# Two blocks of a transformer on one core: the second block's token mixer, cut by token tiles and moved partly beside the first block's expert rows

## The reference

```
h = gelu(einsum('bthkd,btd->bthk', u_tab[idx], xi))
out = einsum('bthk,bthkd->btd', gate * h, v_tab[idx])
```

```
proj = h @ w_in                                     # 1024 x 8208
cb, cc, cu, q, k, v, f_logit, g_conv, g_att = split_cols(proj)
y_conv = short_conv(cb, cc, cu, conv_w, conv_b) @ w_conv_out
s = q @ k.T * scale + (cum[query] - cum[key])       # cum = cumsum(log_sigmoid(f_logit + b)), causal softmax, 16 heads of 64
y_att = o @ w_att_out
return (sigmoid(g_conv) * y_conv + sigmoid(g_att) * y_att) @ w_out
```

## Time and profile before

| | us |
|---|---|
| median of 3 timed runs (2493.71 to 2498.93) | 2497.79 |
| the profiled execution's own time | 2491.84 |
| its span, first to last instruction | 2490.1 |
| PE busy / DVE busy / POOL busy / ACT busy | 1983.1 / 1100.6 / 977.0 / 421.6 |
| PE matmul L2031 (rows of `v`) | 983.7 |
| PE matmul L1840 (weights stationary) | 287.9 and 57.5 |
| HBM read | 857.64 MB |

### The profile page before, as it was taken

How to read it: one execution, slowest core, us unless ns; L and a number is a source line. 1 busy time by engine, 2 the same in 40 slices (tenths; PEclk the granted TensorE clock), 3 DMA queues, 4 the chain that set the end, 5 groups by cost and what they waited for, 6 DMA issues and landing times.

```text
span 2490.1 us, 21117 instructions
## 1 busy us (share of the span) xinstructions
PE 1983.1 (80%) x7462; PEld 1022.2 (41%) x7462; DVE 1100.6 (44%) x2634; ACT 421.6 (17%) x1107; POOL 977.0 (39%) x1059
## 2 busy tenths in 40 slices
PE   8837997779988779989777777789999975566555
PEld 4523552235444225435322222248887732222221
DVE  6579638952457954455975444421012130000001
ACT  2312411201311111311111111101023110000000
POOL 0036757774556775546777777600000000000000
PEclk9868999999999999999999999999989988887887
DMA  6279999999999999999999999966543589999996
GB/s 221 93 262 338 409 402 407 409 409 399 402 357 406 409 409 402 399 372 342 409 409 409 409 409 409 410 208 166 151 101 121 191 342 426 428 426 427 427 427 266
DMA packets 228318, 860.19 MB, mean 345 GB/s; under 512 B 26080, under 2 KB 26592, under 8 KB 216432
## 3 DMA queue, kind: packets, MB, share of 16 engines
q0 software_dynamic: 147456, 536.94, 54.8%
q1 hardware_dynamic: 77488, 312.04, 33.1%
q10 hardware_dynamic: 3264, 9.80, 1.0%
HBM read 857.64 MB, written 1.05 MB: 345 GB/s over the span
## 4 chain that ended last, share of the span: by engine, by line
PE 37%; DMA 28%; DVE 18%; POOL 8%; issue 5%; ACT 2%; SPq 1%; DVEq 0%; ACTq 0%
PE psum L1840 13%; DMA rows<-in_peer_v,idx 8%; PE psum L2031 8%; DVE rows L1051 7%; PE psum L1832 6%; DMA rows<-in_w_e_gate 5%; POOL rows L691 4%; DMA rows<-in_w_e_down 4%; POOL rows L703 4%; DMA rows<-in_peer_u,idx 4%; DMA rows<-in_w_e_up 3%; PE psum L2234 3%; DMA rows<-in_gla_w_in 2%; PE psum L2257 1%; DVE work L934 1%
## 5 line engine op out<-in xcount | busy, mean ns | idle before, releaser
L2031 PE MATMUL psum<-rows,diag 128*128 128x512 f32 x2024 | 983.7, 625 | 264.6 <-ACT diag L1559 136.7
L1051 DVE CUSTOM_DVE_ANT_0 rows<-rows,psum 128x1024 f32<-128x1024 f32 x512 | 614.8, 1220 | 294.0 <-DMA rows<-in_peer_u,idx 283.2
L2031 PEld LDWEIGHTS psum<-rows,diag 128*128 128x128 f32 x2024 | 370.1, 195 | 832.1 <-issue 508.2
L691 POOL DMA_INDIRECT rows<-in_peer_u,idx x512 | 489.5, 956 | 378.2 <-DVEq L728 144.7
L703 POOL DMA_INDIRECT rows<-in_peer_v,idx x512 | 483.7, 945 | 272.6 <-PE psum L2031 148.6
L1840 PE MATMUL psum<-work,rows 128*128 128x256 f32 (+1 forms) x1664 | 287.9, 335 | 0.7 <-ACT work L1378 0.7
L1840 PEld LDWEIGHTS psum<-work,rows 128*128 128x128 f32 x1664 | 260.4, 193 | 31.0 <-issue 5.8
L1559 ACT ACTIVATE diag<-ident,wgt 128x128 f32<-128x128 f32 x506 | 166.0, 389 | 332.1 <-DVE wgt L1059 332.1
L2234 PE MATMUL psum<-rows,work 128*32 128x512 f32 x896 | 136.2, 693 | 106.0 <-DMA kept<-in_w_e_up 46.4
L1321 DVE TENSOR_TENSOR work<-kept,psum 128x512 f32<-128x512 f32 x8 | 8.2, 1030 | 423.2 <-PE psum L2234 423.2
L1378 ACT ACTIVATE work<-psum 128x512 f32<-128x512 f32 (+4 forms) x158 | 81.2, 532 | 547.7 <-PE psum L1840 194.9
(11 more groups left out here) (309 smaller groups left out, 1342.9 us busy)
## 6 DMA issues: line engine op xcount, KB each, us to landing
rows<-in_w_e_up SPq DMA_DIRECT2D x28, 2048.0 KB, 20.1
rows<-in_w_e_gate SPq DMA_DIRECT2D x25, 2048.0 KB, 20.5
rows<-in_w_e_down SPq DMA_DIRECT2D x24, 2048.0 KB, 20.9
rows<-in_w_in SPq DMA_DIRECT2D x32, 1024.0 KB, 9.6
rows<-in_gla_w_in SPq DMA_DIRECT2D x24, 1024.0 KB, 18.4
rows<-in_peer_w_query SPq DMA_DIRECT2D x16, 1024.0 KB, 9.2
rows<-in_peer_u,idx POOLq DMA_INDIRECT x512, 11.7
rows<-in_peer_v,idx POOLq DMA_INDIRECT x512, 12.1
```

The source lines that it names most:

```text
L691: pool.indirect_dma_start(out=u_rows[:, n % RU, :], out_offset=None, in_=a["peer_u"][g // 2], in_offset=bass.IndirectOffsetOnAxis(ap=idx[: ...
L1051: V_.tensor_tensor_reduce(out=u, in0=u, in1=tokens, scale=1.0, scalar=0.0, op0=ALU.mult, op1=ALU.add, accum_out=hid[:, r:r + 1]).then_inc( ...
L2031: last = mm(psum[:, 6 + c, :], diag[:, at % DIAGS, :], v_rows[:, n % RV, c * BANK:(c + 1) * BANK], start=r == 0, stop=summed(n + 1) == sum ...
```

## The change

The stage "mixa" is gone, and "mix" now works on one token tile: ("mix", 0) stands beside the rows of group 3, ("mix", 1) behind them. Every matrix of the mixer is streamed once for each tile, in blocks of 512 columns with the tokens as the stationary side, so that the results stand token by feature; where the next product needs them the other way (`x`, `q`, `k`, `z`, `cb`, the attention's output and `m`), PE transposes them and ACT copies them. 20 blocks of 512 columns and the forget logits belong to each tile. The product of tile 0 with `w_out` is not made in ("mix", 0): it is made at the start of ("mix", 1), as `p0` and `p1`, beside the time in which DVE adds the last experts and norms tile 1. The forget sums are no longer a bias on DVE: each score bank gets a second product (one column of the identity, broadcast, times `cum` of 16 partitions), and DVE takes only the mask. `stage_rows` puts 4 rows behind each of the 20 blocks, 2 behind each set of transposes, 1 behind each `T` and `O` job of the attention and 1 behind `f`: 109 rows.

In ("mix", 1) ACT issues the four first gate matrices of "moe" at four places, behind `k0`, `v1`, `cu1` and `bT1`, after waits for all rows to be used. SP issues the first four up matrices behind the last job of the attention, the last use of ring slot 0, `o0` and `o1`; the final gain waits for `resid1`. SP no longer waits for `u_used`. The `w_out` product of tile 1 is cut in two halves of k over both banks. GpSimd's iota waits for `mT1`. The DVE work of the convolution is the same 24 instructions for each tile, on 128 columns.

```diff
@@ -41,13 +41,12 @@
 
 
 BEFORE = [("mla", 0), ("route", 0)]
-BESIDE = [[("mla", 1), ("route", 1)], [("gla", 0), ("route", 2)], [("gla", 1), ("route", 3)], [("mixa", 0)]]
-AFTER = [("mix", 0), ("moe", 0)]
+BESIDE = [[("mla", 1), ("route", 1)], [("gla", 0), ("route", 2)], [("gla", 1), ("route", 3)], [("mix", 0)]]
+AFTER = [("mix", 1), ("moe", 0)]
 STAGES = BEFORE + [key for beside in BESIDE for key in beside] + AFTER
 
 
-BETWEEN = [{-1: "gc0", 0: "gc1", 1: "gc2", 2: "gc3", 3: "ga0", 4: "ga1", 5: "ga2"},
-           {-1: "ga3", 0: "yc0", 1: "yc1", 3: "oT0_0", 4: "oT0_1"}]
...
-                + ["yc2"] + turned_jobs(1) + ["yc3"] + [f"ya{i}" for i in range(4)] + ["o00", "o10", "o01", "x00", "x01", "o11", "r0"])
+        jobs = (["x0", "x1", "f", "q0", "q1", "k0", "qT0", "qT1", "k1", "v0", "kT0", "kT1", "v1", "cc0", "cc1", "cu0", "cu1",
+                 "cb0", "zT0", "cb1", "zT1", "bT0", "bT1"]
+                + attention_jobs(v, BETWEEN) + ["yc1"] + turned_jobs(v) + ["ya0", "ya1", "mT0", "mT1"])
+        return ["p0", "p1"] + jobs + ["o0", "o1", "x00", "x01", "r0"] if v else jobs
...
-        return {"x01": 2}
+    if stage == "mix":
+        streamed = ["q", "k", "v", "cc", "cu", "cb", "gc", "ga", "yc", "ya"]
+        return {"x1": 2, "f": 1, "qT1": 2, "kT1": 2, "zT1": 2, "bT1": 2, "oT0_1": 2,
+                **{f"{m}{i}": 4 for m in streamed for i in range(2)},
+                **{f"{m}0_{g}": 1 for m in "TO" for g in range(H // 2)}}
     return {"x1": 2, "q": 3, "k": 3, "v0": 3, "v1": 3, "r0": 3, "r1": 3, "low": 1, "gate": 8, "kd": 1, "at": 1,
...
+            out += two("w_out", ["p0", "p1"])
         out.append(("w_in_2", 6 * D, FH, "f"))
-        for m, c in (("cc", 1), ("cu", 2), ("cb", 0), ("q", 3), ("k", 4)):
-            out += two("w_in_2", [f"{m}1", f"{m}3"], c * D)
-        for m, c in (("gc", 6), ("ga", 7)):
-            out += two("w_in_2", [f"{m}1", f"{m}3"], c * D + FH)
-        return out + two("w_conv_out", ["yc1", "yc3"]) + two("w_att_out", ["ya1", "ya3"]) + two("w_out", ["o01", "o11"])
+        for m, c in (("q", 3 * D), ("k", 4 * D), ("v", 5 * D), ("cc", D), ("cu", 2 * D), ("cb", 0),
+                     ("gc", 6 * D + FH), ("ga", 7 * D + FH)):
+            out += two("w_in_2", [f"{m}0", f"{m}1"], c)
+        out += two("w_conv_out", ["yc0", "yc1"]) + two("w_att_out", ["ya0", "ya1"])
+        return out + two("w_out", ["o0", "o1"]) if v else out
     return []
...
                     sp.dma_start(h[:, 1, :], a["x"][P:S, :]).then_inc(h_here[1], 16)
             for n, (key, (what, c0, cols, last, k0, kn)) in enumerate(PIECES):
-                if key == ("mix", 0) and PIECES[n - 1][0] != key:
-
-                    sp.wait_ge(u_used, NU)
                 if n >= NW:
 
                     old_key, old = PIECES[n - NW]
-                    sp.wait_ge(emptied, JOB[(("mix", 0) if old[0] == "mix_gain" else old_key) + (old[3],)])
+                    sp.wait_ge(emptied, JOB[old_key + (old[3],)])
...
+                if at == 4:
+                    sp.wait_ge(emptied, JOB[("mix", 1, "O1_7")])
...
 
-                    for e in (3, 0, 1, 2):
+                    sp.wait_ge(v_used, summed(NU))
+                    sp.wait_ge(v_taken, len(SHARED))
+                    for e in range(GANG):
                         first_free(GANG + e)
                         load_matrix(sp, i, odd, 1, e)
+                    sp.wait_ge(dve_step, STEP["dve"][("moe", 0, "resid1")])
                     sp.dma_start(fin_gain, a["norm_final_g_2"].to_broadcast([P, D])).then_inc(fin_ready, 16)
                 else:
...
                 V("cum", key)
-                V_.memset(x_z[:, :, 0:2], 0.0)
-                got(key, "cu3")
-                link(V_.tensor_tensor(x_z[:, :, 2:], x_cc, x_cu, ALU.mult))
-                for c in range(KD):
-                    link(V_.tensor_scalar(x_cc[:, c, :], x_z[:, c, 0:S], conv_w[:, 0, c:c + 1], conv_b[:, c:c + 1], ALU.mult, ALU.add))
...
                 V("convy", key)
 
-                got(key, f"fb{H // 2 - 1}")
...
+                if t:
+                    act.wait_ge(u_used, NU)
+                    act.wait_ge(v_used, summed(NU))
+                    act.wait_ge(v_taken, len(SHARED))
+                first_gate()
...
+                attend(key, t, x_S, x_pT, x_o, between)
...
+
+                def between(g):
+                    for name in BETWEEN.get(g, []):
+                        if name == "yc0":
+                            seen(key, "convy")
...
+
+                def score(g, banks, w):
+                    for e, hh in enumerate(heads_of(g)):
+                        half = slice(hh % 2 * FD, (hh % 2 + 1) * FD)
+                        mm(banks[e], x_qT[half, hh // 2, :], x_kT[half, hh // 2, 0:w], start=True, stop=False)
+                        pick = ident[0:FH, hh:hh + 1].to_broadcast([FH, P])
+                        last = mm(banks[e], pick, x_cum[0:FH, 0:w], start=False, stop=True)
+                    return last
+
+                if t:
+                    pe.wait_ge(u_used, NU)
+                    got(("mix", 0), "mT1")
+                    for i in range(2):
+                        tokens(f"p{i}", x_mT)
+                seen(key, "xn")
+                for i in range(2):
+                    turned("x", i, x_xn)
+                got(key, "x1")
                 w, bank = Weight(), open_bank(key, "f")
                 for k in range(KD):
-                    last = mm(bank[0:FH, 0:S], w.at(k), x_xT[:, k, :], start=k == 0, stop=k == KD - 1)
+                    last = mm(bank[0:FH, 0:P], w.at(k), x_xT[:, k, :], start=k == 0, stop=k == KD - 1)
                 close(key, "f", last)
-                for m in ("cc", "cu", "cb", "q", "k"):
-                    for i in range(4):
-                        quarter_T(m, i, x_xT)
+                for name in ("q0", "q1", "k0"):
+                    tokens(name)
+                got(key, "q1")
+                for i in range(2):
+                    turned("qT", i, x_q)
+                for name in ("k1", "v0"):
+                    tokens(name)
+                got(key, "k1")
+                for i in range(2):
+                    turned("kT", i, x_k)
+                for name in ("v1", "cc0", "cc1", "cu0", "cu1", "cb0"):
+                    tokens(name)
+                seen(key, "z")
+                turned("zT", 0, x_cc)
+                tokens("cb1")
+                turned("zT", 1, x_cc)
+                got(key, "cb1")
+                for i in range(2):
+                    turned("bT", i, x_cb)
                 seen(key, "cum")
...
+                attend(key, t, score, x_S, x_pT, lambda kt, hh: x_v[:, kt, hh * FD:(hh + 1) * FD], between)
+                tokens("yc1", x_bT)
+                turn(key, t, x_o)
+                got(key, f"oT{t}_1")
+                for i in range(2):
+                    tokens(f"ya{i}", x_oT)
+                seen(key, "m0")
+                turned("mT", 0, x_ya)
+                if t == 0:
+                    seen(key, "m1")
+                    turned("mT", 1, x_ya)
+                    return
+                got(key, "mT0")
+                ws = [Weight() for _ in range(2)]
+                outs = [open_bank(key, f"o{i}") for i in range(2)]
+
+                def out(i, ks):
+                    for k in ks:
+                        last = mm(outs[i], x_mT[:, k, :], ws[i].at(k), start=k == 0, stop=k == KD - 1)
+                    return last
+
+                for i in range(2):
+                    out(i, range(KD // 2))
+                seen(key, "m1")
+                turned("mT", 1, x_ya)
+                got(key, "mT1")
+                for i in range(2):
+                    close(key, f"o{i}", out(i, range(KD // 2, KD)))
                 seen(key, "resid0")
                 for i in range(2):
                     transposes(key, f"x0{i}", chunks(h[:, 0, :], i))
-                out(1, 1)
                 logits(key, 0)
 
             def logits(key, t):
```

More of the change, by code:

```diff
@@ L117, in stage_steps @@
             return ["xn", "abs", "b", "qd", "kd", "at", "state1", "on", "state2", "resid"]
-        if stage == "mixa":
-            return ["xn0"]
         if stage == "mix":
-            return (["xn1", "abs", "cum", "convy", "bias"] + attention_order(0) + attention_order(1)[:4] + ["n0"]
-                    + attention_order(1)[4:] + ["n1"] + [f"m{i}" for i in range(4)]
-                    + ["router", "resid0", "rstd0", "xn0"])
+            head = ["xn", "resid0"] if v else ["xn"]
+            tail = ["rstd0", "m0", "m1", "xn0"] if v else ["m0", "m1"]
+            return head + ["abs", "cum", "z", "convy"] + attention_order(v) + [f"n{v}"] + tail
         return ["resid1", "rstd1", "picked", "shift", "xn1", "keys", "sum0"]
@@ L151, in stage_banks @@
 def stage_banks(stage, v):
-    alone = stage in ("mix", "moe") or (stage, v) == ("mla", 0)
+    alone = (stage, v) in (("mla", 0), ("mix", 1), ("moe", 0))
     return NB if alone else NB_ROWS
@@ L711, in _ @@
```

(41 more changed lines are left out.)

327 lines of the change are left out of this document (133 added, 194 removed).

## The result

The changed kernel takes 2507.45 us (median of 6 runs, 2506.35 to 2511.33); the kernel before, on the same chip, 2498.43 (2493.71 to 2501.61). The ratio is 1.0039, 95% interval 1.0026 to 1.0052: slower by 0.4%, where 2493 was forecast. The profiled execution's span is 2504.5 us against 2490.1, 14.4 longer. The medians differ by 9.0 only: the profiled execution of the kernel before (2491.84) was faster than all six runs of this comparison, that of the changed kernel (2506.35) only 1.1 under its median.

The account below looks back on a forecast made before the run. It took DMA to bound rows and experts, PE the mixer. Group 3 +116, mixer behind it -123.6, step to the experts +3 gave -4.6: 2487.2 us profiled, 2493 as median; range 2466 to 2523.

Parts of the forecast that it names:

- A: Rows of group 3, beside ("mix", 0): the second reading of weights lengthens them by 116 us, bounds 103 to 129.
- rival R1: In group 3, weights cost what they cost in the GLA stage as a whole, 129 us: 2506, slower; chance 0.27.
- B: ("mix", 1), last row to last `w_out` product: 240 us instead of 363.6, so 123.6 us saved.
- rival R3: Granted clock of 0.79 in the 113 us of ("mix", 1) behind `cb1` adds 30 us: 2523; chance 0.10.
- stall: ("mix", 1), `q0` to `cb1`: PE waits 24 us for slow `w_in` weights, bounds 0 to 45.
- The tail: End of ("mix", 1) behind attention, from `yc1` to the products with `w_out`: 39.7 us.
- C: Step from the mixer into the experts: 3 us longer, between 0 and 8.
- Rival R2: Weights keep up in ("mix", 1), no stall, 24 us less: 2469; chance 0.23.

Follow-up runs that it names:

- the picks experiment: Changed kernel with the forget sums' product over all 128 partitions (`cum` zero in 112) instead of 16: 2501.11 us, ratio 1.0015.
- the version with wide picks: Kernel before, with its 32 forget-sum picks over 128 partitions instead of 16, `cum` set to zero first: 2489.92 us, ratio 0.9969.

## Why the prediction was wrong, step by step

**A held.** Group 3 grew by 115.0 us (forecast +116, bounds 103 to 129); the last row came at 1760.8 instead of 1758, the other 2.8 us having come ahead of group 3. The whole-stage price of 129 (rival R1) did not apply. Inside the term, 8.5 us are the row distance. The forecast named it only behind the rows, but the rate that it took from the earlier trace rows is of `w_in` and had it in.

**B is the step that failed:** 255.3 us behind the last row, not 240. Of the 15.3, attention is 11.8 (81.5, not 69.7). It was summed from the earlier trace rows ("32 picks took 10.70 us, 0.33 each, so a pair is 4.1"), as if only the picks were slow and everything else ran as in its rows. Where the clock falls, all that stands there is slow: 16 instructions of a block at 9.10 us instead of 7.03, scores at 1.22 instead of 0.70. With the picks over 128 partitions and the rest as it was, attention took the 69.6 us that the sum had. The mechanism stood in the text as rival R3 with 0.10, from the earlier trace rows, at 0.79 over 113 us and +30; it was 0.81 over 81.5 us and, by the picks experiment, 11.9 us, of which the picks themselves are 3.0 (14.2 against 11.2). What spoke against it, rows at 0.98 with TensorE at 78%, was a stretch of products over 128 partitions and said nothing of 16. The earlier trace rows together held the evidence: a granted clock of 0.86 with TensorE busy for all 50 us leaves waits out as the reason, and the block behind the picks took 9.77 us there against 7.17 for its like in the version with wide picks.

The stretch to the first scores took 132.9 us; the forecast's terms give about 130 (103 to `cb1`, 24 of stall, 3 for the last transposes). The stall was right in size, 21.0 us of waits and some 5 us of slower products behind them (busy 111.6 against 106.6 with fewer waits) for 24, and right in cause: reading from rows 4 KB apart nearly removes it (5.3 us of waits stay, 4.7 of them ahead of the forget product). That the size fits is partly luck: 7.5 of the 21.0 us stood ahead of the forget product, where the forecast had none, and 13.5 behind it.

The sentence of the Trainium skill that the forecast set against it (DMA: Bandwidth & Descriptors, section Latency and other measured facts: with 4 MiB from one partition's row to the next, 4 KiB more restore the rate) does not cover this stride. The page measured distances of 512 KiB and more between neighbouring partitions; in a piece of `w_in` neighbouring partitions read neighbouring rows, 32.8 KB apart, and the 4 MiB that the forecast compared lie between groups of 128 rows. The page has no figure for such a distance, and the forecast's reading of it, no loss, did not hold: 279 against 370 GB/s in two runs of the same pieces is one. The forecast's picture of the start was wrong in one point: it let the first `w_in` piece go when `p0` is emptied and missed that the gain takes a slot. Undoing that gave 3 us here, where the gates delayed the stream too, and 7.5 where they didn't, each from one trace.

The tail was 40.9 us (39.7). **C** was 4.2 us (3, bounds 0 to 8). The misses are +2.5 (the last row's time), +15.3 and +1.2, in sum the 19.0 us between the forecast's -4.6 and the measured +14.4. On the scale of the medians the miss is 14.5 (2507.45 against 2493), less than 19.0, because the forecast put a median 6.0 us above its profiled execution, and for the changed kernel it lay 1.1 above.

Rival R2 (weights keep up) fell with the waits. The Trainium skill's 341 GB/s for transfers of 1 MB (DMA: Bandwidth & Descriptors, section Bandwidth) stood beside it. The page measured it for transfers issued by GpSimd, and the pieces here come on SP's queue: with rows 4 KB apart that had 370, with 32.8 KB 279. The Trainium skill's rule on the clock (TensorE: Matmul & The Clock Gate, section HAM oscillation: waits for DMA between batches drop it) agrees with the slow products behind the long waits, 3.57 us for the forget product against 1.92; it doesn't reach attention, where TensorE stood idle for 1.4 us of 81.5, all of it waits for ACT.

How products over few partitions lower the clock was not found out: 16 and 128 were tried, nothing between, and scores over 64 run beside both. Why group 3 kept 0.98 as a whole was not tried either. Its picks are over 16 partitions too, of 128 columns instead of 256; behind those of its first two pairs a block also took 8.62 us, behind the later ones 7.13, and there rows of `v` stand between the sets.

## What to carry to other kernels

When a stage is bound by TensorE, read its granted clock in windows before adding up durations, and ask what shape of product runs there: products over a few partitions can cost more around them than in themselves (3.0 of 11.9 us here), and filling them up with zeros to 128 partitions cost nothing here. When a weight is to be read more often, with less TensorE work for each byte, take its rate from a stretch where it runs alone, write the ring out slot by slot with the small pieces in it, and list what else is issued ahead of it. One lag can hide another, as the gain's 3 us alone and 7.5 after the gates had moved suggest: judge a fix again once the next lag is gone.

## What the runs showed of the hardware that had not been expected

- 32 products of a 16-partition operand, 10.70 us as a block; of a 128-partition operand, 7.07. In attention the granted clock went from 0.81 to 0.97 by that alone, with TensorE busy for 80.1 of 81.5 us.
- Pieces of 1.05 MB in 2 KB packets: 370 GB/s where rows are 4 KB apart, 279 where they are 32.8 KB apart (and start off multiples of 4 KB), with the same 6.29 MB of gate matrices beside them; in the slower case slices of 380 and of 150 GB/s alternate.
